# Sample state scaled ahead of its product with the key, and the steps after it moved up, in a hybrid decoder layer

## What is computed

```python
qc = chunks(q) * (DK_B ** -0.5)
kbeta = kc * bc[..., None]
u = jnp.einsum('bhnij,bhnje->bhnie', t_mat, vc * bc[..., None])
w = jnp.einsum('bhnij,bhnjd->bhnid', t_mat, kbeta * jnp.exp(gcum)[..., None])
...
v_new = u_i - jnp.einsum('bhcd,bhde->bhce', w_i, state)
o_i = jnp.einsum('bhcd,bhde->bhce', q_i, state) + jnp.einsum('bhcj,bhje->bhce', qk_i, v_new)
state = state * gt_i[..., None, None] + jnp.einsum('bhcd,bhce->bhde', k_i, v_new)
```

## Time and profile before

| | us |
|---|---|
| median of 3 runs | 1182.35 |
| lowest, highest | 1182.23, 1183.67 |
| the profiled execution, its own time | 1183.6 |
| its span, first to last instruction | 1181.8 |
| PE busy / DVE / ACT / POOL in the span | 1146.7 / 828.2 / 492.8 / 276.2 |

### The profile page before, as it was taken

One profiled execution on the slowest core, in us unless ns is written; L12 is line 12 of the kernel. 1 busy time (PEld: TensorE's weight loads), 2 busy tenths in 40 slices (PEclk: granted clock), 3 DMA queues, 4 the chain that ended last, 5 costly groups with the idle time before them and its releaser, 6 DMA issues.

```text
span 1181.8 us, 24834 instructions
## 1 busy us (share of the span) xinstructions
PE 1146.7 (97%) x8241; PEld 1066.8 (90%) x8241; DVE 828.2 (70%) x2226; ACT 492.8 (42%) x1272; POOL 276.2 (23%) x251
## 2 busy tenths in 40 slices
PE   4999999999999999999999999999999999999997
PEld 4899989998999899989998999899998989999996
DVE  4587578777776777677777776778676877665544
ACT  5544345533543454344434443444344445322211
POOL 0223112311231123113211221222122212221211
PEclk9999999999999999999999999999999999999999
DMA  7243446344635363536253625453545374523263
GB/s 254 88 117 99 146 137 197 101 152 130 206 91 171 111 216 91 181 98 217 84 181 120 204 86 186 124 184 104 178 119 180 109 270 139 161 72 107 72 215 145
DMA packets 86635, 172.63 MB, mean 146 GB/s; under 512 B 14034, under 2 KB 24115, under 8 KB 84979
## 3 DMA queue, kind: packets, MB, share of 16 engines
q1 hardware_dynamic: 85246, 169.92, 45.5%
q10 hardware_dynamic: 1312, 1.59, 0.4%
HBM read 153.17 MB, written 17.44 MB: 144 GB/s over the span
## 4 chain that ended last, share of the span: by engine, by line
PE 88%; DVE 5%; issue 3%; ACT 2%; DMA 1%; SPq 0%; DVEq 0%; ACTq 0%
PE PJ L655 20%; PE PJ L651 11%; PE PJ L652 11%; PE PJ L653 11%; PE PJ L656 10%; PE MX L844 2%; PE PJ L956 2%; PE PJ L957 2%; PE MX L765 2%; PE PJ L958 2%; PE MX L853 2%; PE MX L785 1%; PE PJ L659 1%; DVE kvq L1824 1%; DVE S L1787 1%
## 5 line engine op out<-in xcount | busy, mean ns | idle before, releaser
L655 PE MATMUL PJ<-h,w_hi 128*128 128x512 f32 x1110 | 418.6, 413 | 1.4 <-DVE memx L1427 1.4
L2006 POOL TENSOR_TENSOR w_lo<-w_raw,w_hi 128x512 fp32r<-128x512 f32 x160 | 216.3, 1352 | 795.9 <-ACT w_hi L1029 795.1
L651 PE MATMUL PJ<-h,w_hi 128*128 128x264 f32 (+1 forms) x1216 | 359.7, 296 | 0.0
L652 PE MATMUL PJ<-h,w_hi 128*128 128x264 f32 (+1 forms) x1216 | 345.8, 284 | 0.0
L653 PE MATMUL PJ<-h,w_lo 128*128 128x264 f32 (+1 forms) x1216 | 345.4, 284 | 0.0
L656 PE MATMUL PJ<-h,w_lo 128*128 128x256 f32 x1110 | 311.0, 280 | 0.0
L655 PEld LDWEIGHTS PJ<-h,w_hi 128*128 128x128 f32 x1110 | 209.0, 188 | 44.2 <-DVE w_lo L1396 1.7
L1029 ACT ACTIVATE w_hi<-w_raw 128x512 fp32r<-128x512 f32 x320 | 196.8, 623 | 86.7 <-PE PJ L653 73.5
L652 PEld LDWEIGHTS PJ<-h,w_hi 128*128 128x128 f32 x1216 | 230.5, 190 | 1.5
L651 PEld LDWEIGHTS PJ<-h,w_hi 128*128 128x128 f32 x1216 | 230.2, 189 | 0.3
L653 PEld LDWEIGHTS PJ<-h,w_lo 128*128 128x128 f32 x1216 | 229.2, 188 | 0.0
(11 more groups left out here) (320 smaller groups left out, 1680.4 us busy)
## 6 DMA issues: line engine op xcount, KB each, us to landing
w_raw<-in_w_in SPq DMA_DIRECT2D x256, 256.0 KB, 2.8
w_raw<-in_w_out SPq DMA_DIRECT2D x64, 256.0 KB, 2.9
kvq<-in_cache_win_k SPq DMA_DIRECT2D x24, 512.0 KB, 4.7
kvq<-in_cache_win_v SPq DMA_DIRECT2D x24, 512.0 KB, 4.0
mem<-scratch_p SPq DMA_DIRECT2D x24, 512.0 KB, 7.0
out<-memx SPq DMA_DIRECT2D x16, 260.0 KB, 4.8
mem<-in_x_prompt SPq DMA_DIRECT2D x4, 1024.0 KB, 10.1
gx<-scratch_dk SPq DMA_DIRECT2D x8, 512.0 KB, 6.3
```

What stands on the lines that cost most here:

```text
L651: pe.matmul(ps, wh, h_hi[:, k, tok], start=k == 0, stop=False)
L652: pe.matmul(ps, wh, h_lo[:, k, tok], start=False, stop=False)
L655: pe.matmul(both, wh, h2[:, :, k, tok], start=k == 0, stop=False)
L2006: pool.tensor_tensor(w_lo[:, par, 4 * q:4 * q + 4, :], w_raw[:, q, :, :], w_hi[:, par, 4 * q:4 * q + 4, :].bitcast(F32), ALU.subtract).the ...
```

## The change

The scaling of S0 by ACT moves ahead of the product with the key, to ACT's steps 33 and 34, and now waits for the load of S0 and for the decay copies; the product waits for the scaling. Since the scaled state is multiplied, the DVE multiplication by the decay (L1778) is gone. The two copies of beta and decay (L1766, L1767) move from step 33 to step 15 of DVE. The multiply-adds go to steps 38 (3 samples) and 39 (5), the products with the query to steps 41 (2 samples), 42 (1), 43 (3) and 44 (2). PE's sum of squares moves from step 49 to 47, ACT's scale from it from 49 to 48. SP's and POOL's instructions and their order stay as they are. Behind the first lines of the diff, line numbers after are larger by one to three (L1676 and L1680 become L1678 and L1682, L1740 becomes L1742; L1787 stays).

```diff
-                yield from idle(14)
+                yield from idle(12)
                 pe.wait_ge(s["d_vec"], h + 1)
...
             def delta_decode(h):
-                yield from idle(36)
-                act.wait_ge(s["d_sum"], h + 1)
-                rsqrt(dd[:, 9:11, :], MD[:, 1, 0:2 * NB].rearrange("p (a b) -> p a b", a=2), 1.0, s["d_rs"])
-                yield
-                act.wait_ge(s["d_ks"], h + 1)
+                yield from idle(33)
+                act.wait_ge(s["q_row"], 3 * h + 1)
+                act.wait_ge(s["S0_in"], 16 * h + 16)
                 for b in range(NB):
                     last = act.activation(S0[:, b, :], S0[:, b, :], ACT.Copy, scale=dd[:, 11, b:b + 1])
                     if b == 3:
                         yield
                 last.then_inc(s["S0_scaled"], 1)
-                yield from idle(11)
+                yield
+                yield
+                act.wait_ge(s["d_sum"], h + 1)
+                rsqrt(dd[:, 9:11, :], MD[:, 1, 0:2 * NB].rearrange("p (a b) -> p a b", a=2), 1.0, s["d_rs"])
+                yield from idle(12)
...
-                if not first:
+                if first:
+                    dve.wait_ge(s["gates_act"], 5)
+                else:
                     dve.wait_ge(s["qrow_out"], 192 * h)
+                dve.tensor_copy(bt_s(0), bgs[:, 0, h, :])
+                dve.tensor_copy(bt_s(1), bgs[:, 1, h, :])
                 dve.transpose(qrow[:], xk[:, TT - 32:TT]).then_inc(s["q_row"], 1)
...
-                dve.tensor_copy(bt_s(0), bgs[:, 0, h, :])
-                dve.tensor_copy(bt_s(1), bgs[:, 1, h, :])
                 yield
                 yield
                 dve.wait_ge(s["dk_in"], 16 * h + 16)
-                dve.wait_ge(s["S0_in"], 16 * h + 16)
+                dve.wait_ge(s["S0_scaled"], h + 1)
                 yield from fused(s["d_ks"], k_rows, q_rows, dd[:, 0], (5,))
...
-                link(dve.tensor_tensor(dd[:, 6, :], dd[:, 6, :], bt_s(1), ALU.mult))
...
-                yield from idle(4)
-                dve.wait_ge(s["S0_scaled"], h + 1)
+                yield
                 for b in range(NB):
                     last = dve.scalar_tensor_tensor(S0[:, b, :], k_rows[:, b * P:(b + 1) * P], dd[:, 4, b:b + 1],
                                                     S0[:, b, :], ALU.mult, ALU.add)
-                    if b in (2, 4):
+                    if b == 2:
                         yield
                 last.then_inc(s["d_add"], 1)
                 yield
+                yield
                 dve.wait_ge(s["d_add"], h + 1)
                 dve.wait_ge(s["dq_in"], 16 * h + 16)
-                yield from fused(None, q_rows, q_rows, dd[:, 1], (3, 6))
+                yield from fused(None, q_rows, q_rows, dd[:, 1], (2, 3, 6))
                 yield
...
-                yield from idle(3)
+                yield from idle(5)
...
-                ch.at(h, 1, 49)
+                ch.at(h, 1, 48)
```

More of the change, by code:

```diff
@@ L1759, in delta_decode @@
                 dve.wait_ge(s["q_silu"], h + 1)
-                if first:
-                    dve.wait_ge(s["gates_act"], 5)
                 dve.tensor_tensor(dd[:, 2, :], kd, kd, ALU.mult)
```

## The result

The changed kernel takes 1186.15 us (median of 9 runs, 1184.44 to 1189.75); the kernel before takes 1182.83 us beside it (9 runs). The ratio is 1.0034 [1.0022, 1.0046], so the change costs 0.34%. In a second measurement it took 1186.64 us against 1182.55: 1.0029 [1.0020, 1.0038]. The two ratios amount to 4.0 and 3.4 us where the forecast had 1.65. Slower is what happened; the range holds the time, but no change had been called likelier than slower (0.46 against 0.38), and the forecast of 1184.0 us was too low.

A forecast was written before the change was run, and what follows sets the result against it. PE bounds the kernel (busy 1146.7 of 1181.8 us), so only its waits count. Eight heads times 0.2 us add 1.6 us to the span, 1183.4; the same added to the median gives 1184.0 us, range 1179.0 to 1188.0.

The forecast's parts named there:

- Steps 33 and 34: Scaling on ACT: its second four delay POOL's low part and U of level 1; new wait of 0.33 us at level 2.
- The sign that I named: In the profile after, L844 of level 2 has an idle time of 0.2 to 0.4 us before it.
- Steps 37 to 42: Multiply-adds to query products: turns with POOL and `q_rows` put T at 464.24 to 464.5, level 4 at 464.80 to 465.1.
- rivals 1 and 3: Rival 1: levels 4 and 5 on time, 1175, chance 0.15; rival 3: level 2 not late, 1183, within forecast's 0.48.
- The first half of rival 2: Third multiply-add loses its turn to POOL at 457.72: 0.54 us a head, 1186.7; whole rival's chance 0.33.
- Steps 43 to 46: Two query products instead of three ahead of T of level 4: level 5 follows level 4 by 5.64 us, not 5.77.
- Per head: Net against before: +0.18 to +0.46 us, less 0.13, so +0.05 to +0.33 us; 0.2 taken.
- The second half of rival 2: `q_rows` lands at 464.5, level 4 at 465.5: 0.78 us a head, 1188.6; whole rival's chance 0.33.
- Head 0: First head: rope product ahead of T before and after, comes out alike; counted among eight heads at 0.2 us.
- Behind the heads: From the last head to the end: no term in the sum, which was eight heads times 0.2 us.
- The sum: Whole kernel: eight heads times 0.2 us, +1.6 us on a span of 1181.8; median forecast 1184.0 us.

The follow-up runs named there:

- The edit at step 33: Changed kernel with all eight scalings of S0 at ACT step 33 instead of 33 and 34; 1183.81 us, ratio 1.0000 to the kernel before.
- multiply-adds at 42: Kernel before with its multiply-adds one step later (steps 42 to 44) and its query products one step shorter; 1182.35 us, ratio 0.9997.
- one `yield`: Changed kernel with its products with the query one step later (steps 42 to 45); 1179.37 us, ratio 0.9967 to the kernel before.
- load at step 40: Changed kernel with the load of `q_rows` two steps later, at SP step 40; 1223.62 us (2 runs), ratio 1.0339 to the kernel before.

## Why the prediction was right and where it was not

**Steps 33 and 34: right.** A new delay of 0.33 us at level 2 was forecast, 0.28 came. U of level 1 ends at 450.48 (forecast 450.59), the first product with the key, behind POOL's level product, really runs from about 450.89 (450.97; the next one starts at 451.10, 0.21 us behind), T starts at 451.95 (452.08), all in a head that began 0.09 us earlier. The edit at step 33 takes exactly this away. The sign that I named, an idle time shown ahead of L844, isn't in the row; the distance of 6.40 us shows it.

**Steps 37 to 42: right.** Multiply-adds 457.05 (457.11), low part 457.66 (457.72), T of level 2 457.84 (457.92); multiply-adds end at 461.13 (461.14); U of level 3 462.26 (462.36); load issued 459.85 (459.90); first query product 463.57 (463.8); T 464.11 (464.24 to 464.5); L844 464.67, or 464.76 by before's clock (464.80 to 465.1), which is just under the lower bound. So rivals 1 and 3 fell: DVE's idle time was filled, and turns and the load took its place. The first half of rival 2 fell too: the third multiply-add of head 3 kept its turn. The Trainium skill, SBUF — State Buffer, section Who interferes with whom, spoke against the change by the exclusion of such pairs; the 1.35, 0.76 and 1.37 us of U and of products beside POOL agree with it, and so does the low part of 1.62 us in the other direction.

**Steps 43 to 46: wrong by the term of 0.13 us.** Level 5 was to follow in 5.64 us, since two products stand ahead of T instead of three. It follows in 5.78, as before. Behind the products stands the reduction L1429 (L1427 before), and it starts 4.01 us behind L844 of level 4 in both kernels, here in the rows of before and then of after:

```profile
468.42 0.28 DVE L1740 CUSTOM_DVE_ANT_0 q_rows<-S,q_rows 128x128 f32<-128x128 f32 x1
468.63 0.08 DVE L1740 DVE_READ_ACCUMULATOR2_ANT dd<- 128x1 f32 x1
468.63 0.68 DVE L1427 TENSOR_REDUCE memx<-PJ 128x256 f32<-128x512 f32 x1
```

```profile
468.26 0.28 DVE L1742 CUSTOM_DVE_ANT_0 q_rows<-S,q_rows 128x128 f32<-128x128 f32 x1
468.47 0.08 DVE L1742 DVE_READ_ACCUMULATOR2_ANT dd<- 128x1 f32 x1
468.68 0.69 DVE L1429 TENSOR_REDUCE memx<-PJ 128x256 f32<-128x512 f32 x1
```

Before, the reduction starts right behind the third product, together with the read of its sum. After, it starts 0.21 us later than the same pattern would give (468.47). PE isn't what it waits for: the product of PE that it reads, L659, was done at 464.41. The product ahead of it is now the last of the eight, and `fused` closes with `link`, by which DVE waits at once for its own last instruction: the trace has that semaphore at 468.56 and the reduction 0.12 us behind it, and so it is in heads 1 to 7 of both traces of the changed kernel. Before, that closing wait stood at step 46, behind T. So the product saved ahead of T (0.21 us) is paid back by the wait that moved there with it. I had taken T's lateness for the sum of the instructions ahead of it, without asking for the waits between them.

**Per head: right on balance, and partly by luck.** +0.09 to +0.14 us by the distance of heads where the load lands in time, +0.22 in the mean of the first trace and +0.32 of the second, forecast +0.05 to +0.33 with 0.2 taken. Level 4 came 0.14 us later than before where 0.18 to 0.46 was forecast, and the 0.13 us that level 5 should have given back did not come: the two misses offset each other. The second half of rival 2, a late landing, is not a case of its own but happens head by head: in the range I had it as all or nothing.

**Head 0: wrong in size.** The sum took it at 0.2 us as one of eight ("comes out alike"), and overlooked that its load can be late as well. It landed after 4.87 us in the first trace; level 4 came 7.52 us behind level 3 (6.69 before), and with level 2 and 3 head 0 cost 1.14 us. In the second trace the load landed after 3.91 us, and head 0 cost 0.18.

**Behind the heads: not seen.** Of the 0.77 us from head 7 to the end, 0.15 is head 7's own as in the other heads; 0.6 us is lost behind them. The largest piece, 0.40 us, is in the last stage. The rows of ACT and PE there, of before and then of after:

```profile
1012.88 0.39 ACT L1349 ACTIVATE mem<-PJ 128x256 f32<-128x256 f32 x1 [5.74 <-PE PJ L958]
1013.15 0.62 ACT L1029 ACTIVATE w_hi<-w_raw 128x512 fp32r<-128x512 f32 x1
1015.37 0.39 ACT L1349 ACTIVATE mem<-PJ 128x264 f32<-128x264 f32 x1 [1.59 <-issue]
...
1015.41 0.28 PE L958 MATMUL PJ<-h,w_lo 128*128 128x256 f32 x1
1015.81 0.39 PE L956 MATMUL PJ<-h,w_hi 128*128 128x264 f32 x1
```

```profile
1013.64 0.38 ACT L1351 ACTIVATE mem<-PJ 128x256 f32<-128x256 f32 x1 [5.74 <-PE PJ L958]
1016.01 0.63 ACT L1029 ACTIVATE w_hi<-w_raw 128x512 fp32r<-128x512 f32 x1 [1.99 <-PE PJ L958]
1016.55 0.37 ACT L1351 ACTIVATE mem<-PJ 128x264 f32<-128x264 f32 x1
...
1016.17 0.28 PE L958 MATMUL PJ<-h,w_lo 128*128 128x256 f32 x1
1016.97 0.39 PE L956 MATMUL PJ<-h,w_hi 128*128 128x264 f32 x1 [0.52 <-ACT mem L1351]
```

ACT stands still for 1.6 to 2 us in both. Before, it had its high part done and stood in front of L1349; now it stands in front of L1029, and L1351 comes the length of that instruction later. From L958 to L956 PE takes 0.80 us instead of 0.40, and its wait of 0.52 us is in the row. Over all thirteen traces, the matmul L956 has no such wait in the two whose ACT code is that of before (before itself, and multiply-adds at 42), and one of 0.5 to 1.1 us in each of the eleven whose ACT code was changed. So it comes with the edit of ACT's program. From L844 of level 6 in head 7 to the end it is 239.4 and 239.7 us in the two, and 239.5 to 241.2 us in the eleven, 240.5 in the middle. This wait is only a part of that difference; the rest I can't place.

What stops ACT is no semaphore: the releaser named after, PE, is one that had let the same instruction go 0.27 us behind L1349 before. The traces also hold the DMA packets that load program code (kind "instruction"). In each of the thirteen, one of 8 KB starts 1.49 to 1.57 us ahead of ACT's restart (1013.87 for 1015.37 before, 1014.52 for 1016.01 after). That speaks for ACT waiting for its own code; no run takes it away, so it stays an inference from the times.

**The sum.** 1.14 + 1.12 + 0.10 + 0.77 is 3.1 us in the first trace, against 1.6. Heads 1 to 7 are as forecast (1.4 us of the 3.1, against 7 times 0.2); head 0, taken at 0.2 us like the others, cost 1.14, and what stands behind the heads, set at nothing, 0.6. The mechanism of the waits was right, and these two terms decided between no change and slower.

## What to carry to other kernels

When two engines can hold each other, write the order out instruction by instruction and give each its turn; that was right within 0.15 us over 18 us of program. But when work is taken out ahead of a late instruction, look for the waits between the instructions that are left, an engine's wait for itself included, and when a load is moved next to its use, let its landing vary in every repetition, the first included. A late instruction is helped most by what is put behind it: one `yield` was worth 0.7% where the larger move had cost 0.3%. The larger move had made the room: with the scaling at 33, moving the multiply-adds to steps 38 and 39 and the products to 42 and later is worth 0.4%.

## What the runs showed of the hardware

PE idle for 3.80 us (load at step 40) came back at a granted clock of 0.50, which is 1.2 GHz, for 3 us of full work, and was at 0.99 in the 4 us behind that; level 4 to 5 took 1.4 us more. So it went in all eight heads of that run, with waits of 2.92 to 4.60 us ahead of level 4 and 7.09 to 8.26 us from there to level 5. Such a wait costs more than itself: 4.8 us a head here for a load issued 3.2 us later. An idle time of 2.03 us in head 0 of the changed kernel was followed by a clock of 1.00, as were those of 1.12 and 1.22 us in its second trace. But the length alone does not tell. Behind the heads, PE is idle for 2.11 us in the kernel before, and the clock is 0.50 in the 3 us that follow; all thirteen traces have some 3 us at 0.50 there:

```profile
971.31 0.55 PE L956 MATMUL PJ<-h,w_hi 128*128 128x256 f32 x1 [2.11 <-DVE h L1885]
...
969.30:971.30 2.00, 0.00 (x0) 0.02 (x1) 2.00 (x9) 0.52 (x2) 0.00 (x0) 1.00 0.29 51
971.30:974.30 3.00, 2.99 (x14) 3.00 (x15) 3.00 (x7) 2.70 (x7) 0.00 (x0) 0.50 0.98 337
```

POOL's low part is held as well as holding: 1.27 to 1.33 us in the rows of before, 1.41 us where multiply-adds came just ahead of it, 1.62 where U and a product had. The load of 512 KB into `q_rows` took 3.5 to 4.9 us from issue to landing in one and the same kernel.
